# First block: norms, turning and scaling of the first row tile inside the mixers' stage, those of the second tile beside the output product

## The reference

```python
y_conv = _conv_branch(...) * silu(z_conv)      # 256 wide
y_mla = _mla_branch(...) * silu(z_mla)         # 512 wide: 8 heads of causal attention
y_sg = _sgu_branch(...) * silu(z_sg)           # 256 wide
y = concatenate([_rms_norm(y_conv, g_conv), _rms_norm(y_mla, g_mla), _rms_norm(y_sg, g_sg)], axis=-1)
return x + y @ w_out                           # [256, 1024] @ [1024, 1024]
```

## Time and profile before

| | |
|---|---|
| median of three runs | 2465.78 us |
| the profiled execution | 2462.67 us |
| its span, first to last instruction | 2460.9 us |
| PE matmul busy | 2290.4 us (93%) |
| PE weight load busy | 1991.6 us (81%) |
| DVE busy | 1768.9 us (72%) |
| ACT busy | 1234.5 us (50%) |
| DMA | 202 GB/s over the span |
| mean granted clock of TensorE | 0.975 of full |

### The profile page before, as it was taken

How to read it: one execution, slowest core, us unless ns; L and a number is a source line. 1 busy time by engine, 2 the same in 40 slices (tenths; PEclk the granted TensorE clock), 3 DMA queues, 4 the chain that set the end, 5 groups by cost and what they waited for, 6 DMA issues and landing times. The chain is left out here.

```text
span 2460.9 us, 46389 instructions
## 1 busy us (share of the span) xinstructions
PE 2290.4 (93%) x15836; PEld 1991.6 (81%) x15836; DVE 1768.9 (72%) x3178; ACT 1234.5 (50%) x1967; POOL 299.0 (12%) x285
## 2 busy tenths in 40 slices
PE   6979988986999999998999998899999999999997
PEld 6647746963699999996888887679999999788886
DVE  5764864767458887886677778566887888667776
ACT  4543543555444456564545544634446555454544
POOL 0000000000000000002343530000000000335332
PEclk9989999998999999999999999999999999999999
DMA  7554554756337776666777786234777654877775
GB/s 204 197 206 116 185 220 138 258 221 252 109 134 233 226 216 210 189 184 188 240 243 241 241 255 207 103 130 154 230 227 216 199 185 149 259 241 242 240 241 165
DMA packets 247734, 497.92 MB, mean 202 GB/s; under 512 B 58040, under 2 KB 134072, under 8 KB 244304
## 3 DMA queue, kind: packets, MB, share of 16 engines
q1 hardware_dynamic: 247632, 496.55, 63.1%
HBM read 461.82 MB, written 34.65 MB: 202 GB/s over the span
## 5 line engine op out<-in xcount | busy, mean ns | idle before, releaser
L2657 PE MATMUL psum<-split_operands 128*128 128x512 f32 x3072 | 700.3, 390 | 20.7 <-ACT split_operands L2636 20.7
L2657 PEld LDWEIGHTS psum<-split_operands 128*128 128x128 f32 x3072 | 578.7, 188 | 141.8 <-ACT split_operands L2636 21.0
L2395 PE MATMUL psum<-split_operands 128*128 128x256 f32 x4096 | 541.4, 285 | 8.9 <-ACT split_operands L2429 8.8
L2395 PEld LDWEIGHTS psum<-split_operands 128*128 128x128 f32 x4096 | 508.5, 191 | 10.4 <-ACT split_operands L2429 10.4
L2621 POOL TENSOR_TENSOR arena<-arena,residual_gates 128x256 f32 (+1 forms) x256 | 284.9, 1113 | 1750.7 <-DMA residual_gates<-expert_activations 1750.7
L2648 DVE TENSOR_TENSOR split_operands<-weights_ring,split_operands 128x1024 fp32r<-128x1024 f32 x256 | 314.4, 1228 | 203.3 <-ACT split_operands L2636 203.3
L2636 ACT CAST split_operands<-weights_ring 128x1024 fp32r<-128x1024 f32 x256 | 269.5, 1053 | 347.3 <-PE psum L2657 345.8
L2472 DVE TENSOR_TENSOR split_operands<-weights_ring,split_operands 128x1024 fp32r<-128x1024 f32 x256 | 313.2, 1224 | 100.4 <-ACT split_operands L2429 99.5
L325 PE MATMUL psum<-split_operands 128*128 128x256 f32 x2496 | 310.4, 286 | 9.6 <-DVE split_operands L341 6.2
L325 PEld LDWEIGHTS psum<-split_operands 128*128 128x128 f32 x2496 | 305.3, 194 | 16.5 <-DVE split_operands L341 8.5
L2399 PE MATMUL psum<-split_operands 128*128 128x256 f32 x2048 | 288.1, 283 | 0.0
(11 more groups left out here) (320 smaller groups left out, 2011.5 us busy)
## 6 DMA issues: line engine op xcount, KB each, us to landing
weights_ring<-in_peer_u_dram SPq DMA_DIRECT2D x256, 512.0 KB, 3.6
weights_ring<-in_peer_v_dram SPq DMA_DIRECT2D x256, 512.0 KB, 4.4
expert_activations<-residual_gates SPq DMA_DIRECT2D x256, 128.0 KB, 1.8
residual_gates<-expert_activations SPq DMA_DIRECT2D x256, 128.0 KB, 4.1
split_words<-in_w_ada_dram SPq DMA_DIRECT2D x20, 768.0 KB, 6.6
weights_ring<-in_w_in_dram SPq DMA_DIRECT2D x6, 2048.0 KB, 9.0
weights_ring<-in_hg_w_in_dram SPq DMA_DIRECT2D x5, 2048.0 KB, 8.2
arena<-in_hg_w_in_dram SPq DMA_DIRECT2D x5, 2048.0 KB, 7.9
```

What stands on the lines that cost most here:

```text
L2395: nc.tensor.matmul(K.ps[:, 4 + b, 0:SEQ], u_t[:, b, 0, k], h[:, wh, k], start=(k == 0 and wh == 0), stop=False)
L2657: return K.nc.tensor.matmul(K.ps[:, 4 + 2 * t + half], g[:, s, w, t * P:(t + 1) * P], vs[:, s % 2, wv, half * 512:(half + 1) * 512], start ...
```

## The change

The per-branch statistics, the diagonals and the softmax sums get a place of their own (in K.low, which is free by then) that outlives a stage. In `stage_mixers` ACT squares the convolution and spatial-gate branches of both tiles and the attention branch of tile 0, and takes the root for tile 0; DVE runs `heads_out(0)` ahead of `probabilities_out(2)`, makes the diagonals of tile 0 behind it, and scales tile 0 at the end; PE turns tile 0 between `values(2)` and `values(3)`. `heads_out(1)`, the square of the attention branch of tile 1, its root, diagonals, turning and scaling are in the next stage, and PE runs the first group of the output product (tile 0, half 0) ahead of that turning. The scaling is one instruction for a tile in place of eight for both.

```diff
@@ stage_mixers, ScalarE
             exponentials(2)
             exponentials(3)
+            nc.scalar.activation(warm, K.eps[:], ACT.Sqrt)
+            for b, made in ((0, 1), (2, 2)):
+                act.wait_ge(y_made, made)
+                for t in range(TT):
+                    branch_square(K, wide_sq[:, 512 * t + 128 * b:], t, b).then_inc(branch_ms, 1)
+            act.wait_ge(y_made, 3)
+            branch_square(K, wide_sq[:, 1024:], 0, 1).then_inc(branch_ms, 1)
+            act.wait_ge(branch_ms, 5)
+            nc.scalar.activation(M.branch[:, 1, 0], M.branch[:, 0, 0], ACT.Sqrt, bias=K.eps[:]).then_inc(branch_sd, 1)
             mod.act_out(act, 1)
-            nc.scalar.activation(warm, K.eps[:], ACT.Sqrt)
@@ stage_mixers, TensorE
             values(2)
+            pe.wait_ge(diag_ready, 1)
+            turn_rows(K, 0).then_inc(yt_ready, 1)
             values(3)
@@ stage_mixers, VectorE
+            dve.wait_ge(o_ready, 2)
+            heads_out(K, link, 0).then_inc(y_made, 1)
             probabilities_out(2)
-            heads_out(0)
+            dve.wait_ge(branch_sd, 1)
+            branch_diagonals(K, link, 0).then_inc(diag_ready, 1)
             probabilities_out(3)
-            heads_out(1)
+            dve.wait_ge(yt_ready, 1)
+            scale_rows(K, 0)
...
+def turn_rows(K, t):
+    for k in range(KD):
+        b = (0, 0, 1, 1, 1, 1, 2, 2)[k]
+        last = K.nc.tensor.matmul(turned_rows(K)[:, k], K.y[:, t, k * P:(k + 1) * P], K.mix.diag[:, t, b],
+                                  start=True, stop=True)
+    return last
+
+def scale_rows(K, t):
+    return K.nc.vector.tensor_tensor(K.h_t[:, :, t * P:(t + 1) * P], turned_rows(K),
+                                     K.g_branch[:].unsqueeze(2).broadcast_to([P, KD, P]), ALU.mult)
@@ OutProjection.act
+        act.wait_ge(self.heads_made, 1)
+        branch_square(K, self.sq[:, 0], 1, 1).then_inc(self.branch_ms, 1)
+        act.wait_ge(self.branch_ms, 1)
+        K.nc.scalar.activation(st[:, 1, 1], st[:, 0, 1], ACT.Sqrt, bias=K.eps[:]).then_inc(self.branch_sd, 1)
@@ OutProjection.pe
-        pe.wait_ge(self.diag_ready, 3 * TT)
-        ... (16 turning matmuls)
         pe.wait_ge(K.out_loaded, 16 * (self.l + 1))
         for t in range(TT):
             for half in range(2):
+                if t == 0 and half == 1:
+                    pe.wait_ge(self.diag_ready, 1)
+                    turn_rows(K, 1).then_inc(self.yt_ready, 1)
+                if t == 1 and half == 0:
+                    pe.wait_ge(self.y_out, 1)
                 for k in range(KD):
-                    if t == 0 and half == 0:
-                        pe.wait_ge(self.y_out, k + 1)
@@ OutProjection.dve
+        heads_out(self.K, link, 1).then_inc(self.heads_made, 1)
+        dve.wait_ge(self.branch_sd, 1)
+        branch_diagonals(self.K, link, 1).then_inc(self.diag_ready, 1)
+        dve.wait_ge(self.yt_ready, 1)
+        scale_rows(self.K, 1).then_inc(self.y_out, 1)
```

More of the change, by code:

```diff
@@ L474, in mixers_memory @@
     M.end = area.at
+    behind = Area(K.low.rearrange("p c t -> p (c t)"))
+    M.branch = behind.take(3, TT, 3)
+    M.diag = behind.take(TT, 3, P)
+    M.sums = behind.take(TT, HEADS)
     weights = Area(K.arena, 24576)
@@ L733, in stage_mixers @@
         hst = area.take(3, TT, 2 * HEADS)
-        mx, sums = area.take(4, 4), area.take(TT, HEADS)
+        mx, sums = area.take(4, 4), M.sums
         bn, mv, sd, warm = area.take(TT, 6), area.take(TT, 2), area.take(TT, 2), area.take(1)
@@ L743, in stage_mixers @@
         groups = [(t, g) for t in range(TT) for g in range(2)]
+        wide_sq = hsq.rearrange("p n d -> p (n d)")
         w_t = K.glu[:, 0:2].rearrange("p c t -> p (c t)").rearrange("p (g s) -> p g s", g=SG_HEADS)
@@ L761, in stage_mixers @@
         pt_ready, pt_out, o_ready = sem("pt"), sem("pt_out"), sem("o")
+        y_made, branch_ms, branch_sd = sem("y_made"), sem("branch_ms"), sem("branch_sd")
+        diag_ready, yt_ready = sem("branch_diag"), sem("yt")
         sw_ps, mean_ps, var_ps = K.ps[:, 5], K.ps[:, 6, 0:SEQ], K.ps[:, 6, SEQ:2 * SEQ]
@@ L1036, in probabilities_out @@
                 nc.vector.tensor_copy(p_t[n].rearrange("p h a b -> p h (a b)"), s_ps(n)).then_inc(pt_out, 1)
[L1038 to L1045, removed]
             for t in range(TT):
@@ L1095, in _ @@
             dve.wait_ge(pw_out, 1)
-            link(nc.vector.tensor_tensor(K.y[:, :, 0:CONV_W], K.y[:, :, 0:CONV_W], szc, ALU.mult))
+            nc.vector.tensor_tensor(K.y[:, :, 0:CONV_W], K.y[:, :, 0:CONV_W], szc, ALU.mult).then_inc(y_made, 1)
             dve.wait_ge(mix_ready, 1)
@@ L1103, in _, with heads_out, branch_square, branch_diagonals @@
             link(ins)
-            link(nc.vector.tensor_tensor(K.y[:, :, CONV_W + MLA_W:], mixed, u, ALU.mult))
+            nc.vector.tensor_tensor(K.y[:, :, CONV_W + MLA_W:], mixed, u, ALU.mult).then_inc(y_made, 1)
+            dve.wait_ge(o_ready, 2)
+            heads_out(K, link, 0).then_inc(y_made, 1)
             probabilities_out(2)
-            heads_out(0)
+            dve.wait_ge(branch_sd, 1)
+            branch_diagonals(K, link, 0).then_inc(diag_ready, 1)
             probabilities_out(3)
-            heads_out(1)
+            dve.wait_ge(yt_ready, 1)
+            scale_rows(K, 0)
+def heads_out(K, link, t):
+    nc, y, sums = K.nc, K.y[:, t, CONV_W:CONV_W + MLA_W], K.mix.sums[:, t]
+    link(nc.vector.reciprocal(sums, sums))
+    link(nc.vector.tensor_tensor(
+        y.rearrange("p (h d) -> p h d", h=HEADS), K.ps[:, t].rearrange("p (h d) -> p h d", h=HEADS),
+        sums.unsqueeze(2).broadcast_to([P, HEADS, VD]), ALU.mult))
+    return nc.vector.tensor_tensor(y, y, K.rows[:, t, R_ZMLA:R_ZMLA + MLA_W], ALU.mult)
+def branch_square(K, out, t, b):
+    c0, c1 = BRANCHES[b]
+    return K.nc.scalar.activation(out[:, 0:c1 - c0], K.y[:, t, c0:c1], ACT.Square, scale=float(c1 - c0) ** -0.5,
+                                  accum_out=K.mix.branch[:, 0, t, b:b + 1])
+def branch_diagonals(K, link, t):
+    st = K.mix.branch
+    link(K.nc.vector.reciprocal(st[:, 2, t], st[:, 1, t]))
+    for b in range(3):
+        last = K.nc.vector.tensor_scalar(K.mix.diag[:, t, b], K.ident[:], st[:, 2, t, b:b + 1], None, ALU.mult)
+    return last
+def turned_rows(K):
+    return K.ps[:, 2:4].rearrange("p b (k t) -> p (b k) t", t=P)
+def turn_rows(K, t):
[3 more added lines that the diff above has]
+                                  start=True, stop=True)
+    return last
+def scale_rows(K, t):
+    return K.nc.vector.tensor_tensor(K.h_t[:, :, t * P:(t + 1) * P], turned_rows(K),
+                                     K.g_branch[:].unsqueeze(2).broadcast_to([P, KD, P]), ALU.mult)
 BRANCHES = ((0, CONV_W), (CONV_W, CONV_W + MLA_W), (CONV_W + MLA_W, D))
@@ L1122, in __init__ @@
         self.junk = self.sq.rearrange("p t (h n) -> p t h n", h=2)
[L1123 to L1126, removed]
+        self.heads_made, self.branch_ms, self.branch_sd = sem("heads_made"), sem("branch_ms"), sem("branch_sd")
+        self.diag_ready, self.yt_ready, self.y_out = sem("branch_diag"), sem("yt"), sem("y_out")
         self.o_ready, self.x_ready = sem("o_ready"), sem("x_ready")
@@ L1132, in act @@
     def act(self, act):
[L1133 to L1139, removed]
+        K, st = self.K, self.K.mix.branch
+        act.wait_ge(self.heads_made, 1)
+        branch_square(K, self.sq[:, 0], 1, 1).then_inc(self.branch_ms, 1)
+        act.wait_ge(self.branch_ms, 1)
+        K.nc.scalar.activation(st[:, 1, 1], st[:, 0, 1], ACT.Sqrt, bias=K.eps[:]).then_inc(self.branch_sd, 1)
     def pe(self, pe):
         nc, K = self.K.nc, self.K
-        pe.wait_ge(self.diag_ready, 3 * TT)
[L1144 to L1150, removed]
         pe.wait_ge(K.out_loaded, 16 * (self.l + 1))
```

## The result

| | before | changed |
|---|---|---|
| median of six runs, us | 2466.11 | 2442.70 |
| lowest to highest | 2464.33 to 2468.37 | 2438.99 to 2448.48 |
| ratio | | 0.991 (95% interval 0.9896 to 0.9924) |
| profiled execution / its span | 2462.67 / 2460.9 | 2441.18 / 2438.8 |
| mean granted clock | 0.975 | 0.979 |

The change saves 23.4 us by the medians, 18.7 to 25.6 by the interval; 21.3 were forecast.

The account below looks back on a forecast made before the run. PE, busy 93% of the span, was taken as the bound, winnable only where it stands still or runs slowly. Gains of 10.5 and 10.8 us sum to 21.3, from 2465.78 to 2444.5 us, range 2440 to 2451.

Parts of the forecast that it names:

- The end of the mixers on PE: Layer 0, end of second values: 173.90 us against 173.48 before, only 0.42 later, as the added turning fills a gap.
- The diagonals of tile 0: In the mixers: ready at 169.2 us, 0.9 before PE asks at 170.12; any lateness costs PE one for one.
- The scaling: VectorE's last job in the mixers, shown in no row: 1.23 us taken, up to 3.5 if the strided write is slow.
- The seam: Between mixers and output product: 0.56 us from VectorE's end to the next instruction, so the product starts at 174.46.
- the diagonals of tile 1: Behind the seam: 4.1 us with signals, under the product's first quarter of 6.9, slack 2.8 us.
- The gains: Earlier end of the output product: 10.5 us in layer 0 and 10.8 in layer 1, 21.3 together.
- The late `mod.act_out`, the stores and the weights: Layer ends: copies end near 169.5, stores land near 172, before 173.9; weights arrive in time, by 4.4 us in layer 1.
- what would show it: Trace signs: 0.6 to 0.8 us from values 3 to product, ends near 203.9 and 398.7, clock 1.00 throughout.
- (a): Rival: clock falls at the seam all the same, costing 1.7 to 6.0 us, 2446.2 to 2450.5; chance 0.18.
- (b): Rival: new mixers work delays PE through late diagonals, scaling or stores; 3 to 8 us, 2448 to 2452; chance 0.10.
- (c): Rival: half clock through the product, a layer 18.8 us slower; 2474 for one layer, 2503 for both; chance 0.03.
- (d): Rival: later weights of the next products hide the gain beyond 4.4 us of slack; 2447 to 2455; chance 0.03.

Follow-up runs that it names:

- turn_early: Changed kernel with PE's turning of tile 0 ahead of both values instead of between them; one run, 2444.24 us.
- turn_late: Changed kernel with PE's turning of tile 0 behind both values instead of between them; one run, 2451.07 us.
- fill: Kernel before, with extra unread identity matmuls where PE waits at each layer's end; 2454.11 us against 2464.74, ratio 0.9959.
- tile0_filled: tile0_only with 14 extra unread matmuls in PE's wait behind the seam; 2448.99 us against 2463.70 before, ratio 0.9938.
- tile0_only: Changed kernel, but PE turns tile 1 ahead of the whole output product; 2453.13 us against 2464.74 before, ratio 0.9955.
- tile1_only: Changed kernel, but mixers as before: both tiles normed, turned and scaled behind the seam; 2465.18 us against 2464.74 before, ratio 1.0001.

## Why the prediction was right

The forecast was 2444.5 us with 2440 to 2451, the measured median 2442.7. By its steps:

- The end of the mixers on PE, 5.61 us behind the start of the values of group 2: measured 5.57, from 169.65 to 175.22, at a clock of 1.00. The added turning does fill the gap between the values.
- The diagonals of tile 0, forecast 0.9 us ahead of PE: 1.1. turn_early shows that this cover is real and small: asked for one place earlier, they cost 0.87 us.
- The scaling, the operation no row showed, taken at 1.23 within 1.23 to 3.5: 1.22. Had it been 0.5 us longer it would have set the seam; turn_late shows what the seam costs when it does.
- The seam, 0.56: 0.44 and 0.45. Before, VectorE came last and the 0.56 were its way through it; now PE comes last. For layer 1 the prediction took over the 0.56 of layer 0, where its own seam before was 0.97 (rows below this list).
- Behind the seam, the diagonals of tile 1 in 4.1 us with 2.8 of slack: 3.67 and 3.3.
- From the values of group 2 to the product's end, 5.61 + 0.56 + 27.63 + 1.78 = 35.58: 35.51 in both layers. The gains, 10.5 and 10.8: 10.61 and 10.83. The two ends make 21.4 of the 23.4 us between the medians; the other 2 are within the interval and the scatter.
- The late `mod.act_out`, the stores and the weights cost nothing: ScalarE's copies end at 169.88 (forecast 169.5), and no wait for w_in stands in front of its casts.

VectorE's last and ScalarE's first instruction at the seam of layer 1 before, 370.24 to 371.21:

```profile
369.55 0.69 DVE L1045 TENSOR_TENSOR arena<-arena 128x512 f32<-128x512 f32 x1
...
371.21 0.42 ACT L1136 ACTIVATE arena<-arena 128x256 f32<-128x256 f32 x1 [7.18 <-PEq L114]
```

Worked out with this 0.97 us, the gain of layer 1 would have been forecast at 10.4 us instead of 10.8. The prediction did not argue why the smaller figure should hold, so 0.4 us of the match is luck.

Two sentences under what would show it were wrong. From values 3 to the product 0.6 to 0.8 us were named, and it was 0.44. And the product's ends were put near 203.9 and 398.7 us. The second is in the time of the kernel before: the gain of layer 0 has to come off as well, 398.7 - 10.5 = 388.2. Measured: 205.2 and 389.3, the first 1.3 late because the stretch ahead of it ran 1.4 longer (values of group 2 at 169.65 instead of 168.29).

The gain was summed up as one chain; the experiments split it. Keep the waits and hold the clock (fill): 3.1 us a layer. Then take tile 0's chain out of the wait (tile0_filled): from 43.15 to 39.25, 3.9. Then put a quarter of the product in front of tile 1's chain (the changed kernel): to 35.51, 3.7. Together 10.7. Without the fillers the halves are worth 4.6 (tile0_only) and 0.5 (tile1_only) a layer, 5.1 together: the rest comes only when both waits are gone, as in these two kernels the wait left over brought half clock with it, and in tile1_only the turning finds a new wait behind it.

The rivals: (a), a fall of the clock at the seam, did not come in any of six ends of the changed kernel, nor in turn_late with 1.64 us at the seam and both narrow values in front. The granted clock fell in waits of 4.25 us (tile0_only), and there it cost 2.3 us a layer, within the 1.7 to 3.0 that the prediction had set for (a). On this the rows of the seam agree with the Trainium skill ("TensorE: Matmul & The Clock Gate", section "Why this matters for your kernels"), that it is the long idle gaps to be rid of. The fall at 172.5 in the kernel before, behind gaps of 0.51 and 0.82 us, stays outside that rule. fill, with both values at full clock and gaps of 1.11, 1.19 and 1.52 us behind them, shows only that PE's added work there prevents this fall; its cause is open.

(b) did not occur: the diagonals were 1.1 us early, the scaling was at its lower price, and the stage's end was PE's. turn_early and turn_late show what late diagonals and a late scaling cost, 0.9 and 1.4 us a layer. (c), half clock through the whole product, occurred in no run. Nearest to it is tile1_only's layer 1: a first quarter of 9.05 us instead of 7.10, 2 us of (c)'s 29.4, and the clock rose within it. (d) did not occur.

## What to carry to other kernels

A chain of small steps over three engines in front of a large product was worth most moved as a whole (10.7 us a layer, its halves 4.6 and 0.5): cut the work by row tiles, send one tile's chain ahead under other work, and let the product of that tile cover the other's. Half of such a move may show nothing, as tile1_only did, where the wait that was left still had half clock behind it; filling a wait with idle matmuls and comparing the interval around it tells how much of it is clock. When the total scatters by more than the effect, compare an interval between two landmarks on one engine: here it repeated to 0.01 us in three profiles, where runs of the whole kernel lie 9 us apart.

## What the hardware showed that was not expected

- Dummy matmuls in a wait that cannot be shortened made the kernel faster: 7.5 and 10.6 us less in two sets, of which 6.1 are seen in the traces, as values and turning at full clock. The rest is not explained.
- One instruction on VectorE that multiplies 128x1024 out of PSUM with a broadcast gain and writes it in strides took 1.22 us, the same as the plain copy of that size, and less than the old four pairs of 0.88 us for both tiles together (2.44 against 3.5).
- A wait of 4.25 us cost 2.3 us more behind it: 1.8 in the turning that followed and the rest in the product (28.21 us instead of 27.63). With the same wait filled by 14 idle matmuls both were at full clock.
